# Top-k decode in bf16 pairs, pick transposes and gate batches four tiles later, and TensorE's head loop written out

## The reference

```python
q = (xb @ w_query).reshape(t, PEER_HEADS, 2, PEER_HALF)
scores = jnp.einsum('thpd,hpnd->thpn', q, sk)
s_val, s_idx = lax.top_k(scores, PEER_TOPK)
cand = s_val[:, :, 0, :, None] + s_val[:, :, 1, None, :]
c_val, c_idx = lax.top_k(cand.reshape(t, PEER_HEADS, PEER_TOPK * PEER_TOPK), PEER_TOPK)
i1 = jnp.take_along_axis(s_idx[:, :, 0], c_idx // PEER_TOPK, axis=-1)
i2 = jnp.take_along_axis(s_idx[:, :, 1], c_idx % PEER_TOPK, axis=-1)
expert = i1 * N_KEYS + i2
gate = jax.nn.softmax(c_val, axis=-1)
act = jax.nn.gelu(jnp.einsum('thkd,td->thk', expert_u[expert], xb))
out = jnp.einsum('thk,thkd->td', gate * act, expert_v[expert])
```

## Time and profile before

| | us |
|---|---|
| runs | 2912.77, 2910.23, 2913.03; median 2912.77 |
| the profiled execution | 2910.07 |
| its span, first to last instruction | 2908.2 |
| PE busy | 2851.8 (98%), 14716 matmuls |
| PEld busy | 1532.3 (53%) |
| DVE busy | 2315.6 (80%) |
| ACT busy | 1017.2 (35%) |
| POOL busy | 734.6 (25%) |
| granted TensorE clock, mean over the span | 0.993 of full speed |
| DMA | 775.57 MB, 267 GB/s |

### The profile page before, as it was taken

One profiled execution on the slowest core, in us unless ns is written; L12 is line 12 of the kernel. 1 busy time (PEld: TensorE's weight loads), 2 busy tenths in 40 slices (PEclk: granted clock), 3 DMA queues, 4 the chain that ended last, 5 costly groups with the idle time before them and its releaser, 6 DMA issues.

```text
span 2908.2 us, 39928 instructions
## 1 busy us (share of the span) xinstructions
PE 2851.8 (98%) x14716; PEld 1532.3 (53%) x14716; DVE 2315.6 (80%) x4246; ACT 1017.2 (35%) x1347; POOL 734.6 (25%) x518
## 2 busy tenths in 40 slices
PE   8999999989999999999999899999989999999998
PEld 4456555556666444444544455555556664444443
DVE  6855899998888899999401248999988888999995
ACT  2163232325554333333321233232245543333332
POOL 0000232320113444544000001323301124554440
PEclk9999999999999999999999999999999999999999
DMA  4213677767998999999221135677769989999992
GB/s 154 87 46 139 237 275 272 283 251 243 312 311 305 403 392 399 394 399 386 79 87 58 75 122 221 260 279 279 263 239 322 309 290 404 395 395 396 398 398 110
DMA packets 210538, 775.57 MB, mean 267 GB/s; under 512 B 15461, under 2 KB 97513, under 8 KB 190345
## 3 DMA queue, kind: packets, MB, share of 16 engines
q1 hardware_dynamic: 45824, 416.87, 37.5%
q0 software_dynamic: 73728, 268.47, 25.1%
q10 hardware_dynamic: 90888, 89.14, 8.8%
HBM read 681.88 MB, written 92.54 MB: 266 GB/s over the span
## 4 chain that ended last, share of the span: by engine, by line
PE 71%; DVE 20%; DVEq 3%; issue 2%; DMA 2%; ACT 1%; PEld 1%; PEldq 0%; POOL 0%; ACTq 0%
PE ps L1704 32%; PE ps L1631 6%; PE ps L1632 6%; PE ps L1633 6%; DVE arena L1048 5%; PE ps L1324 5%; PE ps L1315 4%; PE ps L1344 4%; DVE arena L1021 4%; PE ps L1605 2%; DMA arena<-in_ur,arena 2%; PE ps L1684 2%; PE ps L1683 1%; DVE arena L1132 1%; DVE arena L1136 1%
## 5 line engine op out<-in xcount | busy, mean ns | idle before, releaser
L1704 PE MATMUL ps<-arena 128*128 128x512 bf16 x4608 | 995.7, 379 | 1.8 <-DVE arena L1199 1.5
L470 POOL DMA_INDIRECT arena<-in_ur,arena x256 | 334.3, 1306 | 1618.3 <-DVE arena L1048 936.9
L1704 PEld LDWEIGHTS ps<-arena 128*128 128x128 bf16 x4608 | 450.5, 98 | 546.2 <-ACT arena L687 2.5
L1021 DVE TENSOR_TENSOR arena<-arena 128x1024 bf16<-128x1024 f32 x512 | 612.3, 1220 | 115.0 <-ACT arena L687 106.8
L1631 PE MATMUL ps<-xnh,arena 128*128 128x384 bf16 x2048 | 668.6, 326 | 2.9 <-issue 2.9
L1633 PE MATMUL ps<-xnh,arena 128*128 128x384 bf16 x2048 | 668.7, 327 | 0.0
L1632 PE MATMUL ps<-xnl,arena 128*128 128x384 bf16 x2048 | 668.7, 326 | 0.0
L687 ACT ACTIVATE arena<-arena 128x1024 bf16<-128x1024 f32 x512 | 525.2, 1048 | 180.7 <-PE ps L1704 115.5
L470 POOL DMA_INDIRECT arena<-in_v,arena x256 | 399.4, 1560 | 406.0 <-DVE x_res L1057 342.1
L1057 DVE SCALAR_TENSOR_TENSOR x_res<-arena,x_res 128x1024 f32<-128x1024 f32 x256 | 328.6, 1283 | 20.8 <-issue 0.5
L1048 DVE CUSTOM_DVE_ANT_0 arena<-arena 128x1024 f32<-128x1024 f32 x256 | 305.7, 1218 | 26.1 <-DMA arena<-in_ur,arena 25.3
(11 more groups left out here) (195 smaller groups left out, 2320.8 us busy)
## 6 DMA issues: line engine op xcount, KB each, us to landing
arena<-in_v SPq DMA_DIRECT2D x64, 2048.0 KB
arena<-in_u SPq DMA_DIRECT2D x62, 2048.0 KB
h_scratch<-arena ACTq DMA_DIRECT2D x60, 768.0 KB
arena<-h_scratch SPq DMA_DIRECT2D x60, 768.0 KB, 8.5
arena<-gate_scratch SPq DMA_DIRECT2D x64, 640.0 KB, 6.8
arena<-in_wmix SPq DMA_DIRECT2D x15, 2048.0 KB, 7.8
gate_scratch<-xnT ACTq DMA_DIRECT2D x10, 2048.0 KB
gate_scratch<-arena ACTq DMA_DIRECT2D x10, 2048.0 KB
```

Of the source, the lines that this page charges most:

```text
L470: pool.indirect_dma_start(ring[n % NBUF], None, ur_d[L] if g < P else vr_d[L], at).then_inc(gat_in[n % NBUF], 16)
L1021: dve.tensor_tensor(lo[:, s], raw[s // TPG][:, s % TPG], hi[:, s], ALU.subtract).then_inc(lo_ready, 1)
L1704: last = pe.matmul(ps[:, 2 + 2 * tt + dh], c, v[:, TPG * s + q, dh * 512:(dh + 1) * 512], start=False, stop=stop and c is cl)
```

## The change

The decode is done in bf16. The ranks of both sides stand side by side and are copied into pairs (`rank_2`), and so are the indices (`idx_2`, each index twice). One comparison and one multiplication over 2048 elements serve both sides, and the sum over 16 is a tree of additions that halve the number of elements, where there was one reduction for each side. TensorE's heads 1 to 7 are written out. The pick transposes stand behind tile 71 and the gate transposes behind tile 72, each four tiles later than before; the batches run from tile 76 to 123 and leave four plain tiles. ScalarE takes the exponential behind tile 70 and the copies of the picks behind tile 71. The products are dealt out anew: the last head does four fewer, six come between the gates and the first batch, four fewer in the tail, and group 3 does products where it did sums before.

```diff
-B0 = NK // 2 + 8
-HG_GROUP = 3
+B0 = NK // 2 + 12
+HG_GROUP = 4
...
-                    if n == NK // 2 + 3:
+                    if n == NK // 2 + 6:
+                        act.wait_ge(ge_sub, L + 1)
+                        act.activation(ex, ex, ACT.Exp).then_inc(ge_exp, 1)
+                    if n == NK // 2 + 7:
                         act.wait_ge(pick_tr, 3 * L + 1)
                         act.activation(pk[:, 0], ps[:, 6, 0:TD], ACT.Copy)
                         act.wait_ge(pick_tr, 3 * L + 2)
                         act.activation(pk[:, 1], ps[:, 5, 0:TD], ACT.Copy).then_inc(pick_i, 1)
-                        act.wait_ge(ge_sub, L + 1)
-                        act.activation(ex, ex, ACT.Exp).then_inc(ge_exp, 1)
...
-                    dots(2 if h else 0)
+                    dots(2 if late else 0)
+                    dve.drain()
+                    for s in range(2):
+                        dve.tensor_copy(idx_2[:, s], idx[:, :, s].bitcast(U32).unsqueeze(3).to_broadcast([P, TT, TOPK, 2]))
...
-                    dots(1 if h else 0)
+                    dots(1 if late else 0)
...
-                    dots(1 if h else 0)
+                    dots(1 if late else 0)
...
-                    for s in range(2):
-                        r = rank[s].bitcast(U32).unsqueeze(2).to_broadcast([P, TT * TOPK, TOPK])
-                        io = iota[:, 0:TOPK].unsqueeze(1).to_broadcast([P, TT * TOPK, TOPK])
-                        dve.tensor_tensor(eq, r, io, ALU.is_equal)
+                    dve.tensor_copy(rank_2.rearrange("p a c -> p (a c)"), ranks.bitcast(U32))
+                    dve.drain()
+                    dve.tensor_tensor(eq, iota_2[:, 0:TOPK].unsqueeze(1).to_broadcast([P, TT * TOPK, TOPK, 2]),
+                                      rank_2.unsqueeze(2).to_broadcast([P, TT * TOPK, TOPK, 2]), ALU.is_equal)
+                    dve.drain()
+                    dve.tensor_tensor(mul.rearrange("p (x k) r c -> p x k (r c)", x=2 * TT),
+                                      eq.rearrange("p (x k) r c -> p x k (r c)", x=2 * TT),
+                                      idx_2.rearrange("p s t r c -> p (s t) (r c)").unsqueeze(2)
+                                      .to_broadcast([P, 2 * TT, TOPK // 2, 2 * TOPK]), ALU.mult)
+                    ahead(RING * h + 13)
+                    dve.drain()
+                    for src, dst, n in ((mul, half, 8), (half, quarter, 4), (quarter, eighth, 2)):
+                        dve.tensor_tensor(dst.rearrange("p a r c -> p a (r c)"), src[:, :, 0:n].rearrange("p a r c -> p a (r c)"),
+                                          src[:, :, n:2 * n].rearrange("p a r c -> p a (r c)"), ALU.add)
                         dve.drain()
-                        e4 = eq.rearrange("p (a k) r -> p a k r", a=TT)
-                        ix = idx[:, :, s].bitcast(U32).unsqueeze(2).to_broadcast([P, TT, TOPK, TOPK])
-                        dve.tensor_tensor(mul.rearrange("p (a k) r -> p a k r", a=TT), e4, ix, ALU.mult)
-                        if s == 0:
-                            ahead(RING * h + 13)
-                        dve.drain()
-                        last = dve.tensor_reduce(picks[:, s, :, h * TOPK:(h + 1) * TOPK],
-                                                 mul.rearrange("p (a k) r -> p a k r", a=TT), AX, ALU.add)
+                    found = view(A_PICK, 2 * TT, P)[:, :, h * TOPK:(h + 1) * TOPK].rearrange("p x (k c) -> p x k c", c=2)
+                    ends = eighth.rearrange("p (x k) r c -> p x k r c", x=2 * TT)
+                    last = dve.tensor_tensor(found, ends[:, :, :, 0], ends[:, :, :, 1], ALU.add)
...
-                ahead(NK // 2 + 6)
+                for n in range(6, 10):
+                    ahead(NK // 2 + n)
                 dve.wait_ge(ge_exp, L + 1)
...
-                ahead(NK // 2 + 7)
-                ahead(NK // 2 + 8)
+                for n in range(10, 13):
+                    ahead(NK // 2 + n)
+                    dots(2)
                 dve.wait_ge(pick_tr, 3 * L + 3)
...
-                for n in range(NK // 2 + 3, NK):
+                for n in range(NK // 2 + 7, NK):
...
-                        dots(4 if k else 2)
+                        dots(4 if k else 3)
...
-                with pe.Fori(1, PH) as h:
+                for h in range(1, PH):
...
-                for j in range(RING):
+                for j in range(B0 - NK // 2):
                     tile(0, NK // 2 + j)
-                    if j == RING // 2 - 1:
+                    if j == RING - 1:
                         pe.wait_ge(topk_done, PH * (L + 1) + 1)
...
-                    if j == RING // 2:
+                    if j == RING:
                         pe.wait_ge(ge_ready, L + 1)
...
-                for j in range(RING):
-                    tile(0, NK - RING + j)
+                for j in range(B0 + NB, NK):
+                    tile(0, j)
```

More of the change, by code:

```diff
@@ L139, in view @@
                 return v
-            names = "abcd"[:len(shape)]
+            names = "abcde"[:len(shape)]
             return v.rearrange(f"p ({' '.join(names)}) -> p {' '.join(names)}", **dict(zip(names[1:], shape[1:])))
@@ L208, in build @@
         gbc = view(o + 4096, D)
-        eq = view(o + 3072, TT * TOPK, TOPK)
-        mul = view(o + 4096, TT * TOPK, TOPK)
+        eq = viewb(o + 3072, TT * TOPK, TOPK, 2)
+        mul = viewb(o + 4096, TT * TOPK, TOPK, 2)
+        half = viewb(o + 3072, TT * TOPK, TOPK // 2, 2)
+        quarter = viewb(o + 3072 + 512, TT * TOPK, TOPK // 4, 2)
+        eighth = viewb(o + 3072 + 768, TT * TOPK, TOPK // 8, 2)
         assert o + 5120 <= A_GR
@@ L217, in build @@
         rank = [view(o + 384 + 64 * s, TT * TOPK) for s in range(2)]
+        ranks = view(o + 384, 2 * TT * TOPK)
+        idx_2 = viewb(o + 512, 2, TT, TOPK, 2)
+        rank_2 = viewb(o + 640, TT * TOPK, 2)
         ex = view(o + 512, TT * PH, TOPK)
```

## The result

The changed kernel takes 2886.39 us, the median of four runs (2883.72 to 2887.83), against 2911.50 us for the kernel before (2909.79 to 2913.03, four runs with it). The ratio is 0.9914, with a 95% interval of 0.9899 to 0.9929: it is 25 us faster, 0.9%. The forecast was 2892.0 us with a range of 2882 to 2903. The profiled execution of the changed kernel took 2887.83 us with a span of 2886.0, that of before 2910.07 and 2908.2. The profiled pair shows 22.2 us.

The account below looks back on a forecast made before the run. TensorE, busy 98% of the span, was taken as the bound; -27.3 us for vanished waits + 2 x 3.0 + 0.5 made -20.8 us, taking the median from 2912.77 to 2892.0 us, range 2882 to 2903.

Parts of the forecast that it names:

- The waits that go: TensorE at tile 67 and the pick transposes: waits and the half-rate stretch vanish in both layers, -27.3 us.
- The cause: Head loop: VectorE needs 48.77 us a head, TensorE 46.72, so VectorE falls 2.05 us behind per head.
- Rival D: Decode misses the pair rate; lag grows, tile 67's low part and tile 68 come late; 2909 to 2913 us, chance 0.04.
- The sizes of the decode: VectorE's bf16 decode passes take 1.22, 0.69, 0.42 and at most 0.28 us, saving 2.1 us a head.
- The new wait: First batch: splits behind the gates' exponential delay the load of tiles 80 to 83; TensorE waits 3 us per layer.
- rival C: Gathers slow the load of tiles 80 to 83 and TensorE returns at 1.2 GHz; 2906 us, chance 0.16.
- The V start: After the last batch TensorE waits 0 to 2.5 us for v's load; 1.0 per layer taken in place of 0.8.
- The sum: Whole kernel: -27.3 + 2 x 3.0 + 0.5 = -20.8 us, median 2892.0.
- 2 x 3.0 + 0.5: Waits added in the total: 3.0 us per layer at the first batch, and 0.5 us more.
- Rival B: First batch and V start: new waits don't arise because the load takes its short time; 2884 us, chance 0.21.
- E: Supplying written-out head code costs 0 to 7.3 us for each of 14 bodies; 2921 us at 2.1, chance 0.04.
- At nothing: Written-out head loop, products moved to later groups, and group 4 as first with sums: no time change.

Follow-up runs that it names:

- e1: Changed kernel with the splits of tiles 74 to 76 and their six products ahead of VectorE's wait for the gates' exponential; 2879.40 us, ratio 0.9904.
- e4: Kernel before with only the bf16 decode put in; 2884.51 us, ratio 0.9916.
- e3: Changed kernel with the fp32 decode of before, all else as changed; 2906.72 us, ratio 0.9995.
- e0: Changed kernel run again without any edit, on another chip than the first follow-ups; 2885.66 us, ratio 0.9919.
- e2: Changed kernel with TensorE's heads 1 to 7 as a hardware loop again; 2884.31 us, ratio 0.9914.
- e6: Changed kernel with the four products of the last head put back there; 2885.42 us, ratio 0.9917.
- e8: Changed kernel with splits and six products ahead of VectorE's wait for the exponential, and the head loop kept; 2879.35 us, ratio 0.9899.
- e5: Changed kernel with four products, not two, between the splits of tiles 74 and 75, six in all as before; 2890.11 us, ratio 0.9943.

## Why the prediction came out as it did

**The waits that go: right.** -27.3 us were forecast. Tile 67 was due at 641.94 and starts at 642.02, the pick transposes at 661.4 and start at 661.52, without a wait, and the clock is full there. With e1, which has no waits left, the two stages sum to 1303.97 us against 1333.25: 29.3 is what there was to have: the 27.3, the 1.5 at the V start, and 0.5 that aren't placed.

**The cause: right.** The lag was read from the earlier trace rows as VectorE's 2.05 us too many per head. e4 removes only that and has the whole gain; e3 leaves only that in and has none. The prediction said of the transposes that "even without any saving in the decode the four tiles and the four products would cover it". In e3 they don't wait, so the sentence holds for them, but what it suggests, that either part alone would bring the gain, doesn't: the lag of the splits sits in the loads as well, and TensorE pays 12.9 us at tile 68, besides the new wait at tile 76. Rival D had this mechanism; the forecast's own part did not.

**The sizes of the decode: right.** 1.22, 0.69, 0.42 and 0.28 us were taken, 1.225, 0.692, 0.426 and 0.29 measured, 0.22 for the casts. The Trainium skill, "VectorE: DVE Perf Modes", section "Mode 2×_1P — pack two bf16 into one 32-bit read", asks for 16-bit elements at step 1; the trace agrees that the pair rate is reached with runs of two, and that the last addition, which writes fp32, is no cheaper (292 ns) than one of twice its elements in bf16 (293 ns). The decode was to end at 639.8; its last instruction ends at 639.2. The gathers, which the copies might have held up, show 1.346 us an issue in the head stretch instead of 1.305, and TensorE has no wait there. Whether the copies make this difference isn't shown.

**The new wait: right in its place, too small for one execution and too large for the median.** The chain was as forecast: exponential done at 660.3 (660.1), load issued at 667.09 (666.5 to 666.7), TensorE stopped at tile 76. Forecast were 3 us per layer, and the full clock from the heads to V, which the first profile doesn't show (0.83 from 680 to 690). That profile has 4.4 and 4.3, because the load took 12.5 and 12.2 us from issue to use where the earlier trace rows gave 8.6 to 11.7, and because TensorE came back at half rate, which was in the sum only for rival C. But e0 has 3.7 and 1.1 in all, e2 1.8 and 1.5, e6 3.7 and 1.1, each above 652.0 with the V start in it. So 3.0 fits layer 0, whose costs run from 1.8 to 4.7, and is too much for most executions of layer 1.

**The V start: too dear.** 1.0 us per layer was taken in place of 0.8; 0.16 and 0 were measured (in e6 1.0 in both layers together). With X = 913.67, v's load was issued at X + 1.7 (1.9 was taken) and first used at X + 12.9 (12.2 to 15.3), and TensorE was ready at X + 17.05 (17.1). The range of 0 to 2.5 us was right, and the load came near its short end; 1.0 was a middle value for which no row spoke more than for 0.

**The sum.** By the first profile: -27.3 + 8.6 - 1.3 = -20.0, near the forecast -20.8 and the 20.3 of the two stages; 2 us more came in untouched code, and against the profiled executions the median of before lies 1.4 us higher and that of the changed kernel 1.4 lower. By e0, e2 and e6 the stages save 24.4, 26.0 and 24.5 us, which is the 24 to 25 of the medians. So the step that was off is the term "2 x 3.0 + 0.5": 6.5 us were put on for new waits, on top of 27.3; the typical execution has 3.3 to 4.9 in new waits and lets go the 1.5 at the V start: with the mean of the three, -29.3 + 4.3 = -25.0 instead of -20.8. Rival B (2884, no new waits) came nearer in its time, but not by its mechanism: the new waits are there in every profile of the changed kernel, and e8, which has none, is 6.3 us faster than e0 on the same chip. E was refuted by e2.

**At nothing: right.** The head loop (e2) and the moved products (e6). The Trainium skill, "Runtime: NRT & Kernel Launch", section "Instruction fetch mechanics", says that a taken branch can stall the fetch of instructions, when its target isn't among those already fetched, and that kernels prefer to be unrolled where possible. This kernel's eight-tile loop body shows no such cost: 2884.31 with the loop, 2885.66 without, and the instruction queue moved 60 packets instead of 37 with no pause at a head's edge.

**Left open.** Why layer 1's mixer, from its first matmul to the scores, takes 294.68 us before (counted as above), 292.73 in the first profile, 294.50 in e2 and 290.95 in e4, with the same code. It doesn't follow the edits, and no experiment here aimed at it. It limits what one profiled pair can say to about 2 to 4 us. Open too is what makes the load behind the new wait take 9.9 us in one execution and 12.5 in another, and what the later transposes would be worth with the old decode and the splits first.

## What to carry to other kernels

When an engine falls a little behind in every round, the saving that counts is the one that brings its round down to the bounding engine's; moving one point where the lag is paid brought nothing here (e3), because other things, buffers and so loads, hang on the same lag, and because the move made a new wait of its own. When a wait is moved in an in-order engine, list what is queued behind it and follow the longest chain (here split, buffer, 2 MB load, preparation, GELU, matmul): three splits and six products moved ahead of a wait were worth 6 us (e8 against e0), at no cost. A late load shows up under the name of the last engine that passed it on, so a releaser is where to begin, not where to stop.

## What the runs showed of the hardware that was not expected

- TensorE's rate after a short wait isn't decided by the length of the wait alone. After 2.90 us (layer 0) and 2.41 us (layer 1) of the changed kernel, its matmuls came 0.32 us apart, 1.2 GHz, seven and nine times in a row; after 2.75 us in e0, 2.15 us in e6 and 2.91 us at tile 76 of e3's layer 0 they came 0.16 apart at once, 2.4 GHz. After 4.28 us (e5) five came at full rate, and only then ten at half. After 9.64 us and 4.40 us (e3) the rate was halved at once. In all of them the engine had run at full rate before.

The granted clock of e0 from 680 to 690, beside the 0.83 of the changed kernel's first profile above:

```profile
680.00:690.00 10.00, 6.77 (x51) 4.29 (x52) 7.64 (x10) 5.78 (x8) 0.00 (x0) 1.00 0.99 416
```

- The same 2 MB load at the same place of either layer, with the same gathers beside it, took from 9.9 to 12.5 us from issue to first use (667.09 to 679.59 in the first profile, 667.33 to 677.79 in e2, 9.91 in layer 1 of e0). The DMA engines were 0.96 to 0.98 busy in these stretches, fast or slow, at 336 to 352 GB/s. An estimate of a wait behind a load can't be better than that.
